# Gate and up tiles of FFN pairs 4 to 10: both parts of h in one matmul of 512 columns, and the down product dealt out between the tiles

## What is computed

```python
def swiglu(h, w1, w3, w2):
    return (jax.nn.silu(h @ w1) * (h @ w3)) @ w2

h = rms_norm(x, ffn1_norm[l])
x = x + FFN_RESIDUAL_WEIGHT * swiglu(h, ffn1_w1[l], ffn1_w3[l], ffn1_w2[l])   # weight 0.5
...                                                                           # mixer: x = x + ... @ w_out
h = rms_norm(x, ffn2_norm[l])
x = x + FFN_RESIDUAL_WEIGHT * swiglu(h, ffn2_w1[l], ffn2_w3[l], ffn2_w2[l])
return rms_norm(x, final_norm)
```

## Time and profile before

| | |
|---|---|
| median of 3 runs | 543.4 us (542.84 to 543.88) |
| span of the profiled execution, first to last instruction | 541.4 us |
| TensorE busy | 531.4 us (98%), 3633 matmuls |
| TensorE weight loads busy | 489.3 us (90%) |
| VectorE busy | 434.0 us (80%), 661 instructions |
| ScalarE busy | 341.2 us (63%), 559 instructions |
| GpSimd busy | 61.3 us (11%) |
| read from memory | 98.27 MB, 183 GB/s over the span |

### The profile page before, as it was taken

The page is one execution under the profiler, slowest core; times in us unless marked ns, Lnnn a source line. Parts: engine busy times, 40 slices in busy tenths (PEclk is TensorE's granted clock), DMA queues, the critical chain, the costliest instruction groups (busy, mean ns, idle before and its releaser), DMA issues.

```text
span 541.4 us, 9714 instructions
## 1 busy us (share of the span) xinstructions
PE 531.4 (98%) x3633; PEld 489.3 (90%) x3633; DVE 434.0 (80%) x661; ACT 341.2 (63%) x559; POOL 61.3 (11%) x99
## 2 busy tenths in 40 slices
PE   8999999999999999999999999999999999999995
PEld 6999999999999979998888788899999999999994
DVE  6899988888887784877768756779898898888845
ACT  6866646655654664867988864675665655656534
POOL 2002000000000210442741102000000000000014
PEclk9999999999999999999999999999999999999998
DMA  9867766565874417568526244527674467765302
GB/s 269 303 234 243 232 205 221 178 187 197 269 233 157 144 36 216 160 214 282 197 84 227 79 157 155 157 79 253 215 247 151 158 219 232 232 184 178 104 0 79
DMA packets 69966, 99.70 MB, mean 184 GB/s; under 512 B 1941, under 2 KB 55393, under 8 KB 69938
## 3 DMA queue, kind: packets, MB, share of 16 engines
q1 hardware_dynamic: 68336, 94.48, 53.3%
q0 software_dynamic: 1456, 4.59, 2.5%
q10 hardware_dynamic: 146, 0.27, 0.1%
HBM read 98.27 MB, written 1.06 MB: 183 GB/s over the span
## 4 chain that ended last, share of the span: by engine, by line
PE 93%; DVE 2%; ACT 1%; issue 1%; SPq 1%; DMA 1%; POOL 1%; POOLq 0%; ACTq 0%; DVEq 0%
PE bank L1734 29%; PE bank L1735 29%; PE bank L1736 29%; DMA x<-in_x 1%; PE bank L1882 1%; PE bank L2029 1%; PE bank L2030 1%; PE bank L2028 1%; SPq L415 1%; PE bank L2069 1%; DVE x L1189 0%; SPq L406 0%; PE bank L2080 0%; PE bank L2081 0%; PE bank L2044 0%
## 5 line engine op out<-in xcount | busy, mean ns | idle before, releaser
L1734 PE MATMUL bank<-hT_hi,w_hi 128*128 128x256 f32 x736 | 208.6, 283 | 0.0
L1736 PE MATMUL bank<-hT_hi,w_lo 128*128 128x256 f32 x736 | 208.3, 283 | 0.0
L1735 PE MATMUL bank<-hT_lo,w_hi 128*128 128x256 f32 x736 | 208.2, 283 | 0.0
L1165 DVE TENSOR_TENSOR w_lo<-raw,w_hi 128x1024 fp32r<-128x1024 f32 x126 | 154.1, 1226 | 21.1 <-ACT w_hi L666 20.5
L666 ACT ACTIVATE w_hi<-raw 128x1024 fp32r<-128x1024 f32 x126 | 132.2, 1056 | 47.7 <-DMA raw<-in_ffn_w 26.5
L1734 PEld LDWEIGHTS bank<-hT_hi,w_hi 128*128 128x128 f32 x736 | 141.1, 192 | 2.0 <-issue 0.5
L1735 PEld LDWEIGHTS bank<-hT_lo,w_hi 128*128 128x128 f32 x736 | 141.1, 192 | 1.3
L1736 PEld LDWEIGHTS bank<-hT_hi,w_lo 128*128 128x128 f32 x736 | 141.1, 192 | 0.0
L1734 PE MATMUL bank<-w_hi,hT_hi 128*128 128x512 f32 (+1 forms) x176 | 66.0, 375 | 1.6 <-DVE hT_lo L1244 0.9
L1736 PE MATMUL bank<-w_hi,hT_lo 128*128 128x512 f32 (+1 forms) x176 | 63.7, 362 | 0.0
L1735 PE MATMUL bank<-w_lo,hT_hi 128*128 128x512 f32 (+1 forms) x176 | 63.5, 361 | 0.0
(11 more groups left out here) (254 smaller groups left out, 825.1 us busy)
## 6 DMA issues: line engine op xcount, KB each, us to landing
raw<-in_ffn_w SPq DMA_DIRECT2D x54, 1024.0 KB, 5.5
raw<-in_w_in SPq DMA_DIRECT2D x16, 1024.0 KB, 5.6
kv_tok<-in_ffn_w SPq DMA_DIRECT2D x10, 1024.0 KB, 5.8
raw<-in_w_out SPq DMA_DIRECT2D x6, 1024.0 KB, 4.9
x<-in_x SPq DMA_DIRECT2D x4, 256.0 KB, 4.0
kv_tok<-in_ffn_w SPq DMA_DIRECT2D x4, 256.0 KB, 4.8
z_silu<-in_ffn_w SPq DMA_DIRECT2D x4, 256.0 KB, 5.2
norm_w<-cs_heads POOLq DMA_DIRECT2D x2, 512.0 KB, 5.0
```

Of the source, the lines that this page charges most:

```text
L1165: dve.tensor_tensor(lo, src, hi, ALU.subtract).then_inc(half_ready, 1)
L1734: pe.matmul(dst, lhs[0], rhs[0], start=start, stop=False, skip_group_check=True)
L1735: pe.matmul(dst, lhs[0], rhs[1], start=False, stop=False, skip_group_check=True)
L1736: return pe.matmul(dst, lhs[1], rhs[0], start=False, stop=stop, skip_group_check=True)
```

## The change

For pairs 4 to 10 (`WIDE_FROM`) h's two parts lie side by side in `hT_both`, and the high part of a weight tile meets both in one matmul of 512 columns; the low part meets the high part of h in one of 256 columns, added to the right half of the bank. A tile, gate or up, now fills the whole of `GU_BANK`: hi x hi left, the two mixed products right. So ScalarE copies the bank out to `halves` after each tile (`copy_halves`), TensorE waits for that copy before the next tile, VectorE adds the two halves for gate and up in one operation (`add_halves`), and the Silu and the product work from SBUF. The 21 down matmuls of the pair before are dealt out behind the four tiles as 4, 5, 5 and 7, in the order of products 1, 2, 4, 6, 5, 7, 3. The lists of ScalarE and VectorE for these pairs are new. In pair 10 the second tile's gate and up halves are added apart (`add_last`), `down_last` starts with the first tile's half of the products, and `mix_lo(1)` moves behind `product_lo(10, 1)` on VectorE, `mix_hi(1)` behind the last copy on ScalarE. Pairs 0 to 3 keep their lists; TensorE's pairs 2 and 3 are unrolled.

```diff
+WIDE_FROM = 4
+DOWN_ORDER = (1, 2, 4, 6, 5, 7, 3)
+DOWN_PARTS = (4, 5, 5, 7)
...
-        hT_hi = sb("hT_hi", [P, 12, SEQ], f32r)
-        hT_lo = sb("hT_lo", [P, 12, SEQ], f32r)
+        hT_both = sb("hT_both", [P, 12, 2, SEQ], f32r)
+        hT_hi, hT_lo = (hT_both[:, :, j, :] for j in range(2))
...
+        halves = conv_acc[:, :, :].rearrange("p (w j) l -> p w j l", w=2)
...
+            def copy_halves(n, i, odd, kind):
+                f = looped(n, i, odd)
+                if kind:
+                    act.wait_ge(up_done, f + 1)
+                else:
+                    act.wait_ge(gate_done, f + 1)
+                    act.wait_ge(gu_ready, f)
+                act.activation(halves[:, kind, :, :].rearrange("p j l -> p (j l)"), bank[:, GU_BANK, :],
+                               ACT.Copy).then_inc(halves_copied, 1)
+            def silu_sum(n, i, odd):
+                if is_last(i) and odd:
+                    act.wait_ge(last_gate_added, n + 1)
+                else:
+                    act.wait_ge(halves_added, wide_tile(n, i, odd) - n + 1)
+                act.activation(silu_g, silu_g, ACT.Silu).then_inc(silu_ready, 1)
...
             def ffn_step(n, i, parity):
+                copy_halves(n, i, 0, 0)
                 second_hi(n, i - 1, 1 - parity)
-                act.wait_ge(gate_done, looped(n, i, 0) + 1)
+                copy_halves(n, i, 0, 1)
+                silu_sum(n, i, 0)
+                left_hi(n, i, parity)
+                copy_halves(n, i, 1, 0)
                 ffn_hi(n, i + 1, 0, 0)
-                silu(n, i, 0)
                 ffn_hi(n, i + 1, 0, 1)
                 product_hi(n, i, 0, P)
-                left_hi(n, i, parity)
-                sum4_hi(n, i)
-                act.wait_ge(gate_done, looped(n, i, 1) + 1)
                 ffn_hi(n, i + 1, 1, 0)
-                silu(n, i, 1)
+                copy_halves(n, i, 1, 1)
+                silu_sum(n, i, 1)
                 ffn_hi(n, i + 1, 1, 1)
                 product_hi(n, i, 1)
+                sum4_hi(n, i)
...
             def last_step(n):
-                i = FI - 1
+                i = LAST_PAIR
+                copy_halves(n, i, 0, 0)
                 second_hi(n, i - 1, 1)
-                silu(n, i, 0)
+                copy_halves(n, i, 0, 1)
+                last_hi(n, 0)
+                silu_sum(n, i, 0)
+                last_hi(n, 1)
+                copy_halves(n, i, 1, 0)
                 product_hi(n, i, 0)
-                for j in range(2):
-                    last_hi(n, j)
-                fold_copy(n)
+                silu_sum(n, i, 1)
                 if n == 0:
                     mix_hi(0)
+                fold_copy(n)
+                copy_halves(n, i, 1, 1)
+                if n == 0:
                     mix_hi(1)
-                silu(n, i, 1)
                 product_hi(n, i, 1)
...
+            def add_halves(n, i, odd):
+                dve.wait_ge(halves_copied, 2 * wide_tile(n, i, odd) + 2)
+                dve.tensor_tensor(halves[:, :, 0, :], halves[:, :, 0, :], halves[:, :, 1, :], ALU.add).then_inc(halves_added, 1)
+            def add_last(n, kind):
+                dve.wait_ge(halves_copied, 2 * wide_tile(n, LAST_PAIR, 1) + kind + 1)
+                own = halves[:, kind, :, :]
+                dve.tensor_tensor(own[:, 0, :], own[:, 0, :], own[:, 1, :], ALU.add).then_inc(
+                    last_up_added if kind else last_gate_added, 1)
+            def wide_product(n, i, odd):
+                dve.wait_ge(silu_ready, looped(n, i, odd) + 1)
+                dve.wait_ge(gu_split, FT * n + 2 * i)
+                if is_last(i) and odd:
+                    dve.wait_ge(last_up_added, n + 1)
+                dve.tensor_tensor(gu[:, odd, :], halves[:, 1, 0, :], silu_g, ALU.mult).then_inc(gu_ready, 1)
...
             def ffn_step(n, i, parity):
                 second_lo(n, i - 1, 1 - parity)
-                pair_sums(n, i, parity)
-                up_silu(n, i, 0)
+                add_halves(n, i, 0)
+                left_sums(n, i, parity)
+                wide_product(n, i, 0)
+                middle_sum(n, i, parity)
+                left_lo(n, i, parity)
+                ffn_lo(n, i + 1, 0, 0)
                 pair_sum4(n, i, parity)
-                ffn_lo(n, i + 1, 0, 0)
+                ffn_lo(n, i + 1, 0, 1)
+                add_halves(n, i, 1)
+                ffn_lo(n, i + 1, 1, 0)
+                wide_product(n, i, 1)
+                operand_sum(n, i, S3)
+                operand_sum(n, i, S1)
                 product_lo(n, i, 0, P)
-                left_lo(n, i, parity)
-                ffn_lo(n, i + 1, 0, 1)
+                operand_sum(n, i, S2)
+                product_lo(n, i, 1)
+                operand_sum(n, i, S4)
                 sum4_lo(n, i)
-                ffn_lo(n, i + 1, 1, 0)
-                up_silu(n, i, 1)
-                operand_sums(n, i)
                 ffn_lo(n, i + 1, 1, 1)
-                product_lo(n, i, 1)
...
             def last_step(n):
-                i = FI - 1
+                i = LAST_PAIR
                 second_lo(n, i - 1, 1)
-                up_silu(n, i, 0)
+                add_halves(n, i, 0)
+                wide_product(n, i, 0)
+                last_lo(n, 0)
+                add_last(n, 0)
                 product_lo(n, i, 0)
-                for j in range(2):
-                    last_lo(n, j)
+                last_lo(n, 1)
                 if n == 0:
                     mix_lo(0)
+                add_last(n, 1)
+                wide_product(n, i, 1)
+                product_lo(n, i, 1)
+                if n == 0:
                     mix_lo(1)
-                up_silu(n, i, 1)
-                product_lo(n, i, 1)
                 fold_sums(n)
...
+                for j in range(2):
+                    pe.wait_ge(last_ready, 2 * n + j + 1)
+                    pe.wait_ge(gu_split, FT * (n + 1) - 1 + j)
                     for c in range(2):
+                        last_product(n, 0, c, j)
+                for c in range(2):
+                    width = 256 if n + c == 2 else 512
+                    for a in range(0, 512, width):
+                        if a:
+                            pe.wait_ge(fold_copied, 2)
+                        for j in range(2):
+                            last_product(n, 1, c, j, a, width)
...
+            def wide_gate_or_up(n, i, odd, kind):
+                h, slot, _ = ffn_half(n, i, odd, kind)
+                pe.wait_ge(half_ready, h + 1)
+                if odd or kind:
+                    pe.wait_ge(halves_copied, 2 * wide_tile(n, i, odd) + kind)
+                for k in range(KD):
+                    hi, lo = w_cols(slot, k)
+                    pe.matmul(bank[:, GU_BANK, :], hi, hT_both[:, k, :, :].rearrange("p j l -> p (j l)"),
+                              start=k == 0, stop=k == KD - 1, skip_group_check=True)
+                    last = pe.matmul(bank[:, GU_BANK, SEQ:], lo, hT_hi[:, k, :], start=False, stop=k == KD - 1,
+                                     skip_group_check=True)
+                last.then_inc(up_done if kind else gate_done, 1)
+            def down_piece(n, i, first, count):
+                p = PAIRS * n + i + 1
+                start, stop = (isinstance(i, int) and i == e for e in (0, PAIRS - 1))
+                for at in range(first, first + count):
+                    j, k = DOWN_ORDER[at // 3], at % 3
+                    if (j, k) == (1, 0):
+                        pe.wait_ge(left_ready, p)
+                        pe.wait_ge(gu_split, FT * n + 2 * i + 1)
+                    elif (j, k) == (2, 0):
+                        pe.wait_ge(gu_split, FT * n + 2 * i + 2)
+                    elif (j, k) == (4, 0):
+                        pe.wait_ge(sum4_ready, p)
+                    elif (j, k) == (6, 0):
+                        pe.wait_ge(sums_ready, p)
+                        pe.wait_ge(asum_ready, p)
+                    elif (j, k) == (3, 0):
+                        pe.wait_ge(corner_ready, p)
+                    lhs, rhs = operands(n, j)
+                    last = pe.matmul(bank[:, P_BANK[j], :], lhs[k // 2], rhs[k % 2], start=start and k == 0,
+                                     stop=stop and k == 2 and j in (1, 5, 6, 7), skip_group_check=True)
...
+            def wide_step(n, i):
+                first = 0
+                for (odd, kind), count in zip(((0, 0), (0, 1), (1, 0), (1, 1)), DOWN_PARTS):
+                    wide_gate_or_up(n, i, odd, kind)
+                    down_piece(n, i - 1, first, count)
+                    first += count
+                if not is_last(i):
+                    pe.wait_ge(halves_copied, 2 * wide_tile(n, i, 1) + 2)
...
-                with pe.Fori(2, FI - 1) as i:
+                for i in range(2, WIDE_FROM):
                     gate_up_down(n, i)
-                gate_up_down(n, FI - 1)
+                pe.wait_ge(gu_ready, looped(n, WIDE_FROM, 0))
```

(3 more changed lines are left out.)

79 lines of the change are left out of this document (61 added, 18 removed).

## The result

The changed kernel takes 548.15 us (median of 4 runs, 547.21 to 548.55), the kernel before 543.26 (4 runs, 542.84 to 543.88): ratio 1.0081, 95% interval 1.0069 to 1.0093. It is slower by 4.9 us, and the forecast of 543.1 with a range up to 546.2 was wrong. The profiled execution took 547.21 us, with a span of 545.0 from the first to the last instruction (span before: 541.4). In the four runs 2.15 to 2.21 us lie outside the span; in the 51 runs of the kernel before that were timed beside the experiments it is 1.75 to 1.90. So 4.5 of the 4.9 us are lost inside the span and 0.4 outside it.

What follows compares the result with a forecast made beforehand. TensorE's queue was taken to bound the loops: 12 x 0.32 = 3.8 us saved, 2.5 lost at the first seam, 1.0 at the end, sum -0.3. Span 541.1 plus 2.0 outside gave 543.1 us, range 540.2 to 546.2.

Steps and rivals of the forecast that it cites:

- rival E: VectorE's 0.9 or ScalarE's 0.3 us of slack does not hold, each pair loses 0.2: 545.5 us; chance 0.10.
- step k: In a wide tile, one matmul of 512 plus one of 256 takes 0.347 us instead of 0.360.
- rival C: Inside wide tiles, switching widths costs a third of the entry each time, k = 0.356: 546.5 us; chance 0.12.
- A: The forecast as summed, 543.1 us, own range 541.6 to 544.4; chance 0.48.
- the stall: TensorE's wait for ScalarE's copy behind the piece of 4: 0 to 0.10 us per pair, taken as 0.05.
- E: Issue end of a gate tile, zero of the walk: copy until E+0.86, release E+0.9, piece of 4 covers until E+0.92.
- the first seam: Where the first FFN ends and TensorE waits for VectorE and ScalarE: about 2.5 us lost at the transposes.
- (a): First seam: 14 down matmuls instead of 9 ahead of the last tile's end, 0.77 us later.
- (b): First seam: copy and add in place of a Silu ahead of the product, 0.64 us.
- (c): First seam: mix_lo(1), a split of 1.13 us, now on VectorE between gu_lo and the fold sums.
- the end seam: End of the second FFN: (a) and (b) without (c), 1.41 us at the fold sums, 1.0 lost after slack.
- rival D: TensorE idles 3.3 us at the first seam, the clock falls to half: +2.4 to +4.8, 545.5 to 547.9 us; chance 0.08.

Runs made afterwards that it cites:

- e9_free: Kernel before with wide tiles in pairs 4 to 9 alone; pair 10's first tile does not wait for pair 9's last product: 542.42 us.
- e7_grouped: Changed kernel with each tile's eight 512-column matmuls first, then its eight 256-column ones: 546.74 us.
- e10_best: e9_free with each wide tile's 512-column matmuls ahead of its 256-column ones: 540.63 us.
- e1_narrow: Changed kernel with each 512-column matmul split into two of 256 again, wide order of work kept: 551.55 us.
- e2_parts: Changed kernel with down pieces of 5, 5, 5, 6 instead of 4, 5, 5, 7: 555.03 us.
- e3_mixback: Changed kernel with mix_hi(1) and mix_lo(1) of pair 10 back ahead of the last copy and add: 546.78 us.
- e11_mixgroup: Changed kernel with the edits of e3_mixback and e7_grouped at once: 545.33 us.
- e4_keep: Changed kernel with 22 small filler products on TensorE ahead of the transposes of the first seam: 548.85 us.
- e8_fill11: Changed kernel with 11 small filler products on TensorE ahead of the transposes of the first seam: 547.11 us.
- e6_loop: Wide tiles in pairs 4 to 9 alone, pair 10 and its products as in the kernel before: 545.57 us.
- e12_five_four: e10_best with down pieces of 5, 4, 5, 7 instead of 4, 5, 5, 7: 539.78 us.
- e13_waits: e10_best with ScalarE's two waits ahead of a gate tile's copy in the other order: 539.76 us.

## Why the prediction was wrong

**The right bound, the right path.** TensorE's queue in the loops and the chain of VectorE and ScalarE in the seams (where an FFN ends) set the end, as told. What failed are sizes of its terms, and one term that it put at nothing. e9_free shows loops and seams apart. The followers (rival E) kept up: no wait of TensorE for them in the loops.

**Failed: the step k.** "From the nearest rows it is 0.227 + 0.120 = 0.347" holds where each width stands in a run of its own (e7_grouped: 0.346), not in turn (0.351 to 0.354 in all but three of 36 tiles). The changed kernel alternates. The prediction had this as rival C, but only with a third of the entry's cost and 0.356; it lay between A and C. Over 12 pairs this is 12 x 0.13 = 1.6 us.

**Failed: the stall.** The walk from a tile's end to the release was right to 0.1 us (copy start 0.28 behind E, copy 0.60), yet from the ends 0 and 0.10 I took the middle, 0.05. The copy started 0.28 and not 0.20 behind E, which left the piece of four no time to spare, so the row of the first matmul behind a wait (0.10) applied in full and a little more: 0.135 in grouped tiles (2.902 - 2.766). That is 12 x 0.085 = 1.0 us more. The list of waits of the changed kernel has the weight load of that first matmul, not the matmul, waiting for the copy, once in each of the 12 pairs (us in total, times, longest):
```profile
PEld bank L1947 <- ACT conv_acc L842: 3.2, 12, 0.3
```
The Trainium skill (TensorE: Matmul & The Clock Gate, section Step-by-step: what each phase is for) has weight loads pulled ahead; the trace agrees where nothing waits (0.23 to the next start) and not behind the wait (0.32 in the changed kernel, 0.333 in e10_best).

These two account for the loops: 0.13 + 0.085 = 0.215 per pair against the 0.32 forecast leaves 0.105, measured 0.70/6 = 0.117 and 0.65/6 = 0.108.

**Mis-sized: the first seam,** 2.86 instead of 2.5. (a) was 14.62 - 13.57 = 1.05, not 0.77: the four tiles carry the two errors above here as well. (b) was 0.77, not 0.64: from the tile's end to gu_lo 2.30 us against 1.53; most of the excess is the step from the add to the product that reads it, 0.56 (185.15 to 185.71) where 0.45 was taken. (c) was 1.14, as told. Sum 2.96 at the fold sums (188.10), of which 0.10 was slack.

**Mis-sized: the end seam,** 1.31 instead of 1.0, for the same (a) and (b): 1.05 + 0.77 = 1.82, of which 0.51 went in slack on the way.

**Wrong odds: the clock.** The stretch at 1.2 GHz was foreseen as rival D, at 0.08. It came in each of the four traces with about 3.1 us of waiting there (the changed kernel, e1_narrow, e2_parts, e7_grouped), and in neither of the two with 2.1. The mean clocks of all runs show that it does not come in every run, and more often with the longer wait:

| wait at the first seam | runs with a mean clock of 0.994 or less |
|---|---|
| about 3.1 us (the four above) | 18 of 19 |
| 2.1 us (e3_mixback, e11_mixgroup) | 5 of 10 |
| filled (e4_keep, e8_fill11) | 0 of 9 |
| pair 10 as before (the kernel before, e6_loop, e9_free, e10_best, e12_five_four, e13_waits) | 0 of 82 |

A mean does not say where the clock fell; only the traces do. D's mechanism and place were right; its price was not. 2.4 to 4.8 us was reckoned from 12 to 24 matmuls, while 0.73 is what 3.4 us at half clock cost in the trace, and 1.7 to 1.9 what 6.8 us cost. That the other three runs of the changed kernel are longer than the profiled one is probably this second length: their mean clocks and e8_fill11's spans fit. It is not shown, and e7_grouped's own runs speak against a fixed price: the one at 0.998 has a span of 544.5 us, those at 0.992 and 0.993 544.4 to 544.9.

**Put at nothing: the time outside the span.** "2.0 us outside the span, which nothing here touches" set the median of some runs against the span of another execution, and took it as the same for both kernels. In the 82 runs whose pair 10 is as before it is 1.75 to 1.90 us, in all 29 with a wide pair 10 and no filler 2.13 to 2.24. This is 0.4 us of the loss; what takes it is open.

**Together:** loops +2.45 against the forecast, seams +0.36 and +0.31, clock +0.73, the rest +0.1: 3.95 us on a forecast of -0.3 gives +3.66, the difference of the profiled spans. The 0.4 outside the span and the 0.9 by which the usual run is longer than the profiled one (median span 546.0, before 541.5) make it the 4.9 that was measured. No single miss would have left the range. All of them have the same sign, since each term was taken near its favourable end: the sum of two rows for k, the middle for the stall, tiles without either in the seams, and no clock.

**Not settled:** why a 512 between two 256s takes up to 0.24 to the next start and not 0.229. That it goes when the widths are grouped is shown, what in the engine does it is not; and three tiles that alternate in the same order took 2.78 us, which is 0.347 per k. Nor was it tried whether a wide pair 10 could be made to pay with a shorter chain behind it.

## What to carry to other kernels

A saving on the bounding engine is counted where that engine is the bound; ask first what the same edit does to the last iteration, where another chain takes over, and keep the old form there (here 0.2% faster instead of 0.8% slower, and 0.7% faster once the matmuls were grouped and two waits changed places). When a new form frees a resource earlier, look for old waits that still guard it (here 1.34 us of waiting at each of two places), and put the wait that is met last at the end of a row of waits. When the seam gets longer, price the clock too, over several runs and not from one trace. And compare the time outside the span of both kernels before you call it untouched.

## What the runs showed of the hardware

- Matmuls in float32r of 512 and 256 columns in turn: 0.351 to 0.354 us per pair of them; each width in its own run of eight: 0.346 (e7_grouped); three of 256: 0.359 (e1_narrow).
- Two waits in a row on ScalarE, the first met late and the second long before: the instruction starts 0.28 us behind the event; with the late one last, 0.20 (e10_best and e13_waits).
- The first matmul behind the wait for a copy is followed after 0.32 to 0.33 us instead of 0.23 where the copy began 0.28 us behind the tile, and after 0.26 where it began 0.20 behind it (piece of four in both).
- With 3.1 us of waiting on TensorE the clock was at 1.2 GHz for 3.4 or 6.8 us, for 0.7 or 1.7 to 1.9 us behind it. In e7_grouped it fell 1.3 us ahead of the wait's end, in the changed kernel 1.0 behind it. With 2.1 us no trace has such a stretch, but 5 of 10 runs have the mean clock of one. 2.7 us of filler in the 3.1 kept it up in all five runs (mean clocks 0.996 or 0.997).
- The same kernels differ in the time outside the span: 1.75 to 1.90 us with pair 10 as before, 2.13 to 2.24 with a wide one, 2.50 to 3.09 with 11 fillers.
- The first 25 us vary from run to run: the first tile of pair 1 began between 23.01 and 23.56 us in the fourteen traces, whose order of work ahead of it is the same. Differences of spans under 0.5 us are read from a landmark behind it.
